# The convolution module's units moved to the head of the input projection, and its 31-tap sums out of the mixer

## The reference

```
h    = rms_norm(x, g_norm1) * (1 + scale1) + shift1          # scale, shift, gate: silu(c) @ w_ada + b_ada
proj = h @ w_in                                              # q,k,v (12 tiles of 128), z (4), b/a rates, glu_u (4), glu_g (4)
o_a  = gdn_mixer(q,k,v, z, rates)                            # conv of width 4, silu, l2 norm, chunked delta rule
hc   = glu_u * sigmoid(glu_g)                                # conformer module, 512 channels = 4 tiles of 128
y    = causal_depthwise_conv(hc, buf, w_dw)  (31 taps)  + b_dw
o_b  = silu(group_layer_norm(y) * g_ln + b_ln)
x    = x + gate1 * (concat(o_a, o_b) @ w_out)
x    = x + gate2 * feed_forward(rms_norm(x) ...)             # layer 0: dense SwiGLU; layer 1: top-2-of-8 experts
```

## Time and profile before

| | |
|---|---|
| three runs, us | 1968.99, 1996.34, 1996.32 (median 1996.32) |
| profiled execution, us | 1973.2, its span in the trace 1971.4 |
| busy in the span | PE 1777.9 us (90%), DVE 1416.2 (72%), ACT 1083.5 (55%), POOL 100.6 (5%) |
| mean granted TensorE clock | 0.933 of full speed |
| experts of layer 1 | from 905 us to the end, 333 GB/s |

### The profile page before, as it was taken

One profiled execution on the slowest core, in us unless ns is written; L12 is line 12 of the kernel. 1 busy time (PEld: TensorE's weight loads), 2 busy tenths in 40 slices (PEclk: granted clock), 3 DMA queues, 4 the chain that ended last, 5 costly groups with the idle time before them and its releaser, 6 DMA issues.

```text
span 1971.4 us, 26503 instructions
## 1 busy us (share of the span) xinstructions
PE 1777.9 (90%) x9884; PEld 1517.9 (77%) x9884; DVE 1416.2 (72%) x1594; ACT 1083.5 (55%) x1043; POOL 100.6 (5%) x110
## 2 busy tenths in 40 slices
PE   5996687799989956886999999999999999999996
PEld 2885586799988855765888887888878888788885
DVE  2468625554444796265888988888888898888987
ACT  3243144344332531352677677777777776777775
POOL 0002310000000023101000000000000000000000
PEclk8997687899998976977999999999999999999999
DMA  9685112244444740111799999999899998899995
GB/s 388 251 333 225 48 49 86 108 170 167 153 147 171 294 190 29 49 68 61 298 343 359 353 343 347 348 356 359 341 339 346 357 370 333 336 354 355 364 342 204
DMA packets 70052, 499.48 MB, mean 253 GB/s; under 512 B 7952, under 2 KB 7952, under 8 KB 10928
## 3 DMA queue, kind: packets, MB, share of 16 engines
q1 hardware_dynamic: 66384, 481.00, 64.0%
q0 software_dynamic: 3552, 16.87, 2.2%
HBM read 485.79 MB, written 12.05 MB: 253 GB/s over the span
## 4 chain that ended last, share of the span: by engine, by line
PE 84%; DVE 9%; ACT 3%; issue 2%; DMA 1%; DVEq 0%; SPq 0%; ACTq 0%
PE ps L1897 15%; PE ps L1899 15%; PE ps L1898 15%; PE ps L1473 8%; PE ps L1475 7%; PE ps L1474 7%; DVE yc L992 3%; PE ps L1484 2%; DMA raw<-units 1%; PE ps L1842 1%; PE ps L1555 1%; PE ps L1874 1%; PE ps L1569 1%; PE ps L1494 1%; PE ps L1567 1%
## 5 line engine op out<-in xcount | busy, mean ns | idle before, releaser
L923 DVE TENSOR_TENSOR wlo<-raw,whi 128x2048 fp32r<-128x2048 f32 x403 | 920.5, 2291 | 255.1 <-ACT whi L580 252.1
L580 ACT ACTIVATE whi<-raw 128x2048 fp32r<-128x2048 f32 x403 | 772.1, 1917 | 328.8 <-PE ps L1899 220.3
L1897 PE MATMUL ps<-whi,ht_hi 128*128 128x512 f32 x896 | 357.9, 399 | 5.1 <-issue 3.8
L1899 PE MATMUL ps<-whi,ht_lo 128*128 128x512 f32 x896 | 350.8, 391 | 0.0
L1898 PE MATMUL ps<-wlo,ht_hi 128*128 128x512 f32 x896 | 350.0, 391 | 0.0
L1473 PE MATMUL ps<-h_hi,whi 128*128 128x288 f32 x864 | 264.0, 306 | 26.9 <-DVE h_lo L976 25.3
L1474 PE MATMUL ps<-h_lo,whi 128*128 128x288 f32 x864 | 259.2, 300 | 0.0
L1475 PE MATMUL ps<-h_hi,wlo 128*128 128x288 f32 x864 | 258.2, 299 | 0.0
L1473 PEld LDWEIGHTS ps<-h_hi,whi 128*128 128x128 f32 x864 | 166.6, 193 | 50.2 <-issue 48.3
L1897 PEld LDWEIGHTS ps<-whi,ht_hi 128*128 128x128 f32 x896 | 169.0, 189 | 42.5 <-issue 8.9
L1899 PEld LDWEIGHTS ps<-whi,ht_lo 128*128 128x128 f32 x896 | 168.7, 188 | 36.6
(11 more groups left out here) (289 smaller groups left out, 1928.7 us busy)
## 6 DMA issues: line engine op xcount, KB each, us to landing
raw<-units SPq DMA_DIRECT2D x455, 1024.0 KB, 5.5
sst<-gdn_in POOLq DMA_DIRECT2D x8, 512.0 KB, 5.3
gdns_out<-sst POOLq DMA_DIRECT2D x8, 512.0 KB, 2.9
qst_out<-qpad POOLq DMA_DIRECT2D x2, 1890.0 KB, 6.3
cst_out<-cpad POOLq DMA_DIRECT2D x2, 1116.0 KB, 8.4
x<-x_in SPq DMA_DIRECT2D x1, 1152.0 KB, 11.5
y_out<-hf SPq DMA_DIRECT2D x2, 576.0 KB, 3.3
cpad<-cst_in POOLq DMA_DIRECT2D x2, 544.0 KB, 8.7
```

What stands on the lines that cost most here:

```text
L580: act.activation(whi[s % NSPLIT][:, :], raw[u % NRAW][:, :], ACT.Copy).then_inc(hi_split, 1)
L923: dve.tensor_tensor(wlo[s % NSPLIT][:, :], raw[unit_of(s) % NRAW][:, :], whi[s % NSPLIT][:, :].bitcast(F32), ALU.subtract).then_inc(lo_spl ...
L1897: mm(ps[:, bank, :], a_hi[:, a], whi[u % NSPLIT][:, w], start=(first and i == 0), stop=False)
L1899: last = mm(ps[:, bank, :], a_lo[:, a], whi[u % NSPLIT][:, w], start=False, stop=(end and i == 3))
```

## The change

All four convolution units come first (0 to 3), q/k/v are units 4 to 9, and z is 10 and 11. `TAPS_IN` puts all 124 taps into the iterations of `project_in`: 14 in each of iterations 2 to 4, 11 in each of 5 to 10 (beside a `conv_pair`), 16 in iteration 11. `SUMS_IN` puts the four sample sums at the end of the taps in iterations 3, 5, 7 and 9. The mixer's calls of `fill` and `sample_taps` are gone. `fill` itself, `sample_taps`, `conv_pair` and POOL's program are as before.

```diff
--- before.py
+++ after.py
@@ -107,23 +107,18 @@
 
 
 COL_Z, COL_B, COL_U, COL_G = 1536, 2048, 2056, 2568
-I_QKV, I_Z = 2, 2 + QKV_T // 2
-CONF_UNITS = (0, 1, 10, 11)
+I_QKV, I_Z = CT, CT + QKV_T // 2
+CONF_UNITS = tuple(range(CT))
 _conf = [[COL_U + c * P, COL_G + c * P] for c in range(CT)]
-IN_COLS = _conf[0] + _conf[1] + [m * P for m in range(QKV_T)] + [COL_Z + h * P for h in range(H)] + _conf[2] + _conf[3]
+IN_COLS = sum(_conf, []) + [m * P for m in range(QKV_T)] + [COL_Z + h * P for h in range(H)]
 COLUMNS_IN = 316
 N_CONV = QKV_T // 2
 
 
-def taps_in(i):
-
-    convolves = I_QKV < i <= I_QKV + N_CONV
-    return 0 if i < 2 else 3 if convolves else 9
-
-
-
-FILL = (14, 7, 14, 4, 4, 3)
-
+
+
+TAPS_IN = [0, 0] + [14] * 3 + [11] * 6 + [16]
+SUMS_IN = {3 + 2 * c: c for c in range(CT)}
 
 
 SCATTER_AT = range(1, 17, 2)
@@ -1039,7 +1034,9 @@
                         conv_pair(l, i - I_QKV - 1)
                     if i == 1:
                         copy_rates(l)
-                    fill(l, min(taps_in(i), 2 * CK - taps[0]))
+                    fill(l, TAPS_IN[i])
+                    if i in SUMS_IN:
+                        sample_taps(l, SUMS_IN[i])
                     if i in CONF_UNITS:
                         c = CONF_UNITS.index(i)
                         bank = wait_tile((("in", l), i, 0))
@@ -1152,33 +1149,24 @@
 
             def mixer(l):
                 decay_rates(l)
-                fill(l, FILL[0])
-                sample_taps(l, 0)
                 for i in range(2):
                     dve.wait_ge(qrs_ready, 2 * l + i + 1)
                     q3 = kt(qkv, QKV_T)[:, H * i:H * i + H]
                     dve.tensor_tensor(q3, q3, kt(qrs[i], H), ALU.mult).then_inc(qn_ready, 1)
-                    fill(l, FILL[1])
-                    sample_taps(l, 1 + i)
                 dve.wait_ge(eg_ready, l + 1)
                 dve.wait_ge(beta_ready, l + 1)
                 dve.tensor_copy(gcs, ps[:, 0, 0:12])
                 dve.tensor_tensor(bEG, beta, eg[:, 0:12], ALU.mult).then_inc(beg_ready, 1)
                 dve.wait_ge(beg_ready, l + 1)
-                fill(l, FILL[2])
-                sample_taps(l, 3)
                 for b in range(2):
                     differences(l, b, b, P)
-                    fill(l, FILL[3])
                 for b in range(2):
                     products(l, b, b, P)
-                    fill(l, FILL[4])
                 for b in range(2):
                     inverse_start(l, b, b, P)
                 for i in range(len(LEVELS)):
                     for b in range(2):
                         inverse_level(l, b, P, 2 * i + b, LEVELS[i], i == len(LEVELS) - 1)
-                        fill(l, FILL[5] if i == 0 else CT * CK)
                     if i in (2, 4):
                         center_conf(l, (i - 2) // 2)
                     if i == 4:
```

## The result

| | before | changed |
|---|---|---|
| median of 20 runs, us | 1976.9 (1968.8 to 1997.4) | 1968.4 (1964.3 to 1975.8) |
| ratio, 95% interval | | 0.9933 [0.9911, 0.9955] |
| profiled execution, its span, us | 1973.2, 1971.4 | 1969.1, 1967.3 |

The change makes the kernel 0.7% faster, under the 2% that were called telling, but clearly not nothing. The forecast was 1986 us. Against the profiled execution it was 1973.2 - 10 = 1963 us; that of the changed kernel took 1969.1. Three slow executions, two of before at 2121 and 4518 us and one of warm_before at 4543 us, are left out of every comparison.

What follows compares the result with a forecast made beforehand. PE was taken to set the pace in the input projection, with DVE 2.5 us per unit to spare. Layer 0 at -6.7 and layer 1 at -2.9 made about -10, so 1996.3 - 10 = 1986 us, range 1954 to 2002.

Steps and rivals of the forecast that it cites:

- the base: Whole kernel: the median of three runs, 1996.3 us, from which the gain of 10 us was taken.
- Step 1: Input projection: DVE's turns take 9.9 or 11.2 us, the last 8.5; two POOL blocks charged 0.7 us each.
- Step 2: Projection's end: DVE done at 179.2 and 724.1 us; block start -0.6 us in layer 0, +4.2 in layer 1.
- Step 3: Mixer, block start to second level's matmul: 5.9 us less per layer, and 1.2 us less a step further.
- Step 4: State transfers issued by POOL among the weights: 1 us more in layer 0 (0 to 7), nothing in layer 1.
- POOL did not stop DVE for its whole block: Rival, projection: POOL's products stop DVE for the full 4.1 us per block; 16 us more, 2002 us; chance 0.17.
- The sign given for it: Projection: width-4 convolutions of over 4.5 us or splits of over 3 us beside POOL would show POOL stops DVE.
- The cover: Rival, projection: DVE keeps up with PE, block starts 11 and 14 us earlier than Step 2; 1961 us; chance 0.10.
- The clock: Rival, projection: PE's clock at half in units 8 to 11, PE 14 to 17 us late; 2016 us; chance 0.08.

Runs made afterwards that it cites:

- warm_before: The kernel before with 24 idle matmuls per layer on PE in the wait ahead of the dense stage; ratio 0.9988.
- before_a: The kernel before, unedited, run once more for a profile; 1992.5 us.
- pool_quiet: The changed kernel with POOL's sample products cut from 128x248 to 128x8; 1969.6 us, ratio 0.9956.
- taps_behind: The changed kernel with the last 16 taps of the projection moved behind the decay rates; 1962.8 us, ratio 0.9918.
- cover: The changed kernel with 5 taps in each of iterations 5 to 11 and 47 in DVE's idle time in the mixer; 1946.5 us, ratio 0.9842.
- state_late: The changed kernel with POOL's two state transfers behind the masks of the mixer, not in the projection; 1969.0 us, ratio 0.9911.
- cover_late: The cover kernel with POOL's two state transfers behind the masks of the mixer; 1938.5 us, ratio 0.9788.

## Why the prediction was wrong, and where it was right

**The step that failed is the base.** The prediction set the three runs aside with "a spread of 1.4% that nothing in the trace explains" and took "the forecast for the median is 1996.3 - 10 = 1986 us". The median of 20 runs of before is 1976.9. A level near 1996 is that of executions with the long stretch in both layers: before_a, at 1992.5 us and a clock of 0.922, shows 20.8 us of it, and runs of 1997 us had a clock of 0.920. By their times two of the three runs lay there (no profile of them exists); of the 82 executions of before timed beside the other kernels, 37 took 1980 us or more. The trace given was of an execution without one, and its own sum gave 1963 us; the base that agreed with it was 1973. Against the median of 20 the same -10 gives 1967; 1968.4 was measured.

That this comes so near is in part luck. The median of before holds long executions (8 of its 20 took 1980 us or more, none of the changed kernel's), which the sum does not count. Like beside like, the profiled pair gives 4.1 us and the lowest runs 4.5, less than half of the 10. The terms follow.

**Step 1** was mis-sized in POOL's charge: 0.7 us for each of two blocks (bounds 0 to 1.7), measured 1.7 (5.05 against 3.3 us; pool_quiet gives it back). The charge was low because more than half of the block was to fall beside a split. It did, for 2 us, but there POOL stood still; all that DVE lost, it lost in the pair. The right value was the upper end of the bounds, 1.7 us, which the row of the taps showed.

**Step 2** was right in its mechanism: DVE without idle time, PE's wait ahead of the sums of squares. DVE was to be done at 179.2 us; it was at 181.2, and in layer 1 at 721.3, where the split of unit 6 came 4.8 us earlier than before (643.87 for 648.65), so 726.1 against 724.1. Both misses are the 2 us of step 1. Block start: 193.0 for 190.8, and 737.3 for 735.3 by the same count. taps_behind and cover show the cause directly: take taps from that list and the block start follows.

**Step 3** was to give 5.9 + 1.2 us; from the block start to the second block's matmul it gave 30.2 - 22.4 = 7.8. The masks took 1.26 us each, not 1.43, without taps beside them, and the second block's exponential ended 7.9 us behind the block start, not 8.9. At the second level another 1.7 us came (forecast 1.2): 9.5 us in all, in either layer, where the sum had 7.1. At the first centring layer 0 was 7.9 us earlier (forecast 7.7), layer 1 a further 3.7 (forecast 2.9). That layer 0 agrees is luck: the 2.4 us too little here cancel the 2.2 too little at the block start.

**Step 4** charged 1 us for the transfers. They took longer to land, before 6.3 and 8.4 us, and cost nothing (state_late). The page's DMA issues, as in the earlier trace rows:

```profile
qst_out<-qpad POOLq DMA_DIRECT2D x2, 1890.0 KB, 11.8
cst_out<-cpad POOLq DMA_DIRECT2D x2, 1116.0 KB, 16.4
```

So 11.6 us were gained by the first centring of each layer, more than the 9.6 of the sum. 4.1 us are left at the end of the profiled pair: the stretch behind took 2.5 and 1.6 us more, the experts 1.2, the rest small steps. The sum had nothing for what lies behind the centring. The stretch differs in both profiles of the changed kernel (56.7 to 56.8) from both undisturbed ones of before (54.2 to 55.1), yet state_late has 54.4 in one layer; whether it is a price of the change stays open. In the changed kernel and in state_late none of 30 executions had a time above 1976 us, where 37 of 82 of before had 1980 or more. So the long case did not come in them; but pool_quiet and cover, small edits of the same kernel, each show one, and what keeps it away isn't shown.

**The rivals.** POOL did not stop DVE for its whole block. The sign given for it, width-4 convolutions of over 4.5 us, came all the same (5.05); 3.3 and the 1.7 us of the taps' row are already 5.0, so this sign could not tell the rival from the forecast. The cover did not hold, as forecast; cover and cover_late show what it would have been worth, 22 and 30 us. The clock did dip in the projection (0.81 in a window with gaps), hidden behind DVE. What the prediction held against this rival, that the clock was full wherever PE had no gaps, the runs don't bear out: the dip was 3.4 us of unbroken matmuls behind a gap of 2.3 us, and in before_a's mixer the clock was 0.50 through 26 us without a gap.

## What to carry to other kernels

Work moved out of a stage that waits must go where its new engine has time: count the receiving engine's turn against the pace of the stage (here 9.9 and 11.2 us against 9.2), and leave in the old place what the old waits cover; that division was worth more (cover and cover_late, 22 and 30 us) than the move itself (8.5 us). What is free beside a late engine, as 3 MB of transfers here, is not free once that engine is on time. And take the base of a forecast from the execution whose trace was read, not from a median of three whose other levels it doesn't show.

## What the runs showed of the hardware that was not expected

The same instructions, in the same order, run at either clock level from one execution to the next: a dense stage of PE behind a wait took 20 matmuls in 4 us or 38, for 9 to 11 us per layer, and the time of an execution mostly follows its mean granted clock (before: 0.933 at 1973 us, 0.927 at 1986, 0.920 at 1997). Keeping PE busy in the wait kept the clock at 1.00 there, yet in one execution it fell later, in unbroken work; what sets the moment stays open.

POOL and DVE take turns by whole instructions: a 0.67 us product of POOL took 2.60 us behind a running 128x2048 split of DVE and cost it nothing, and 0.43 us where the DVE instruction was the one that came second. What POOL cost DVE here went by the number of DVE instructions that met a product, four per block, and not by POOL's busy time.
